# Rows of maxima and factors brought to all partitions by DMA instead of by matmul, and a new order at the heads' end

## What is computed

```python
b = jnp.cumsum(lf, axis=-1)
d_log = jnp.where(causal, b[..., :, None] - b[..., None, :] + ig[..., None, :], -jnp.inf)
inter_log = b + m[..., None]
m_t = jnp.maximum(inter_log, jnp.max(d_log, axis=-1))
dmat = jnp.exp(d_log - m_t[..., None])
inter = jnp.exp(inter_log - m_t)
s = jnp.einsum('bhtd,bhsd->bhts', q, k) * dmat
num = jnp.einsum('bhts,bhsd->bhtd', s, v) + inter[..., None] * jnp.einsum('bhvd,bhtd->bhtv', C, q)
den = jnp.sum(s, axis=-1) + inter * jnp.einsum('bhd,bhtd->bht', n, q)
h = num / jnp.maximum(jnp.abs(den), jnp.exp(-m_t))[..., None]
```

## Time and profile before

| what | us |
|---|---|
| median of 3 runs | 1875.0 (1872.1 to 1875.5) |
| the profiled execution, whole | 1875.4 |
| its span, first to last instruction | 1873.6 |
| TensorE busy (matmuls, modelled ends) | 1829.5 (98%), 9601 matmuls |
| VectorE / ACT / GpSimd busy | 1045.4 / 521.3 / 261.3 |
| DMA moved | 320 MB, 171 GB/s in the mean |

### The profile page before, as it was taken

The page is one execution under the profiler, slowest core; times in us unless marked ns, Lnnn a source line. Parts: engine busy times, 40 slices in busy tenths (PEclk is TensorE's granted clock), DMA queues, the critical chain, the costliest instruction groups (busy, mean ns, idle before and its releaser), DMA issues.

```text
span 1873.6 us, 25258 instructions
## 1 busy us (share of the span) xinstructions
PE 1829.5 (98%) x9601; PEld 1567.2 (84%) x9601; DVE 1045.4 (56%) x2340; ACT 521.3 (28%) x1054; POOL 261.3 (14%) x229
## 2 busy tenths in 40 slices
PE   6989999999999999999999999999999999999998
PEld 5877889888898888988888888888889888898886
DVE  6686774546636276353853447453673627636373
ACT  3344321332223122222222223132221312222221
POOL 3442222030220002000030001200022000210000
PEclk9899999999999999999999999999999999999999
DMA  9885634594256542664427642466425654266421
GB/s 330 269 307 170 208 101 178 166 308 158 90 183 190 175 152 80 214 191 158 135 91 236 192 168 91 149 212 202 147 82 192 189 179 150 76 216 192 137 97 68
DMA packets 134620, 319.94 MB, mean 171 GB/s; under 512 B 11788, under 2 KB 53476, under 8 KB 134500
## 3 DMA queue, kind: packets, MB, share of 16 engines
q1 hardware_dynamic: 129028, 312.56, 50.6%
q10 hardware_dynamic: 5472, 5.77, 0.9%
HBM read 272.09 MB, written 46.20 MB: 170 GB/s over the span
## 4 chain that ended last, share of the span: by engine, by line
PE 77%; DVE 16%; issue 3%; ACT 2%; DMA 1%; POOL 0%; SPq 0%; ACTq 0%; DVEq 0%; POOLq 0%
PE ps_acc L512 20%; PE ps_acc L514 20%; PE ps_acc L513 20%; PE ps_kv L512 2%; PE ps_kv L513 1%; PE ps_kv L514 1%; PE ps_sco L710 1%; DVE sb_shifted L1609 1%; PE ps_num L525 1%; DVE sb_acc_cv L1466 1%; PE ps_num L738 1%; PE ps_kv L742 1%; PE ps_num L737 1%; DVE sb_hm L1466 1%; PE ps_num L512 1%
## 5 line engine op out<-in xcount | busy, mean ns | idle before, releaser
L512 PE MATMUL ps_acc<-sb_hT_hi,sb_w_split 128*128 128x512 f32 x1536 | 603.3, 393 | 1.3 <-POOL sb_w_split L1092 0.7
L514 PE MATMUL ps_acc<-sb_hT_hi,sb_w_split 128*128 128x512 f32 x1536 | 598.8, 390 | 0.0
L513 PE MATMUL ps_acc<-sb_hT_lo,sb_w_split 128*128 128x512 f32 x1536 | 598.8, 390 | 0.0
L514 PEld LDWEIGHTS ps_acc<-sb_hT_hi,sb_w_split 128*128 128x128 f32 x1536 | 288.6, 188 | 61.4
L512 PEld LDWEIGHTS ps_acc<-sb_hT_hi,sb_w_split 128*128 128x128 f32 x1536 | 289.1, 188 | 59.6 <-DVE sb_oz L1486 1.0
L513 PEld LDWEIGHTS ps_acc<-sb_hT_lo,sb_w_split 128*128 128x128 f32 x1536 | 288.9, 188 | 59.2
L1104 POOL TENSOR_TENSOR sb_h_rs<-sb_h_var,sb_mhalf 128x4 f32<-128x4 f32 x32 | 32.4, 1012 | 1028.7 <-DVE sb_h_var L1560 1028.7
L1092 POOL TENSOR_TENSOR sb_w_split<-sb_w_raw,sb_w_split 128x512 fp32r<-128x512 f32 (+1 forms) x64 | 88.7, 1396 | 187.3 <-ACT sb_w_split L823 187.2
L1466 DVE SCALAR_TENSOR_TENSOR sb_acc_cv<-sb_shifted,sb_par,sb_acc_cv 128x512 f32<-128x512 f32 x96 | 76.9, 801 | 61.0 <-ACT sb_acc_cv L962 58.5
L1492 DVE TENSOR_TENSOR sb_oz<-sb_tanh,sb_oz 128x512 f32<-128x512 f32 x32 | 22.2, 693 | 150.4 <-ACT sb_tanh L978 150.4
L512 PE MATMUL ps_acc<-sb_wo_hi,sb_mixm_hi 128*128 128x512 f32 x256 | 103.1, 403 | 0.0
(11 more groups left out here) (233 smaller groups left out, 2929.1 us busy)
## 6 DMA issues: line engine op xcount, KB each, us to landing
sb_w_split<-w_kept SPq DMA_DIRECT2D x328, 512.0 KB, 3.6
sb_w_split<-w_kept SPq DMA_DIRECT2D x56, 520.0 KB, 4.5
w_kept<-sb_w_split SPq DMA_DIRECT2D x40, 512.0 KB, 5.1
sb_x_res<-x SPq DMA_DIRECT2D x34, 512.0 KB, 5.3
sb_w_raw<-w_in SPq DMA_DIRECT2D x64, 256.0 KB, 4.6
out<-sb_qT SPq DMA_DIRECT2D x32, 512.0 KB, 2.9
sb_x_in<-x SPq DMA_DIRECT2D x30, 512.0 KB, 5.3
sb_ada_raw<-w_ada SPq DMA_DIRECT2D x8, 1024.0 KB, 9.7
```

The lines of the kernel that those rows point to most:

```text
L512: pe.matmul(dst, st_hi, mv_hi, start=start, stop=False)
L513: pe.matmul(dst, st_hi, mv_lo, start=False, stop=False)
L514: return pe.matmul(dst, st_lo, mv_hi, start=False, stop=stop)
```

## The change

- `wide_rows`, `m_wide`, `inter_wide`, `chunk_sel`, `head_mask` and the matmuls L713 and L726 go, with the five instructions of setup that filled them.
- ACT stores `m_row` and `inter_row` to a DRAM tensor after t = 6 (`keep_rows`), waits for both stores after t = 8, and loads, for each chunk, 4 rows of 128 (2 KB) to all 128 partitions: `load_m_row(j)` and `load_inter_row(j)`, 256 KB each, into `m_row_all` and `inter_row_all`. The next chunk's are issued once this chunk's were read: the maxima's before the Exp of dmat, the factors' before the tanh of tile zp.
- The transposes of hm go to bro instead of sco.
- The order at the heads' end is new on VectorE and ACT.

```diff
-SCO = {("qk", 0): 1, ("qk", 1): 2, ("hm", 0): 3, ("qk", 2): 4, ("hm", 1): 5, ("qk", 3): 6, ("hm", 2): 7, ("hm", 3): 8}
+SCO = {("qk", j): j + 1 for j in range(NC)}
...
-        m_wide, inter_wide = sb("m_wide", [P, NH, P], F32R), sb("inter_wide", [P, NH, P], F32R)
-        chunk_sel = sb("chunk_sel", [P, NC], F32R)
-        head_mask = sb("head_mask", [16, NH])
+        m_row_all, inter_row_all = sb("m_row_all", [P, BLK]), sb("inter_row_all", [P, BLK])
+        rows_kept = nc.dram_tensor("rows_kept", [2, 16, P], F32, kind="Internal").ap()
...
     heads_to_scores(j), TensorE
-                    bro_wait(5 + 2 * j)
-                    pe.matmul(bro[:, :], col(chunk_sel, j), m_wide[:, :, :].rearrange("p h t -> p (h t)"),
-                              start=True, stop=True).then_inc(bro_full, 1)
...
     numerator_and_update(j), TensorE
-                    pe.wait_ge(bro_free, b * B_USES + (7 + 2 * j))
+                    pe.wait_ge(q_in_ready, b * NC + (j + 1))
...
                 def hm_transposed(j):
-                    pe.wait_ge(sco_free, b * S_USES + SCO["hm", j])
+                    bro_wait(5 + j)
                     pe.wait_ge(hm_ready, b * NC + (j + 1))
                     for h in range(NH):
-                        last = pe.transpose(sco[:, chunk(h)], hm[:, h, :], ident)
-                    last.then_inc(sco_full, 1)
+                        last = pe.transpose(bro[:, chunk(h)], hm[:, h, :], ident)
+                    last.then_inc(bro_full, 1)
...
                     tile("u", j)
                     keys_transposed(j)
-                    inter_rows(j)
                     tile("zp", j)
...
+                def keep_rows():
+                    act.dma_start(rows_kept[0], m_row[0:16, :]).then_inc(rows_kept_done, 16)
+                    act.wait_ge(inter_row_ready, b + 1)
+                    act.dma_start(rows_kept[1], inter_row).then_inc(rows_kept_done, 16)
+
+                def load_m_row(j):
+                    act.dma_start(m_row_all[:, :], rows_kept[0, NH * j:NH * j + NH, :].rearrange("h t -> (h t)").partition_broadcast(P)).then_inc(
+                        m_row_loaded, 16)
...
+                    if t == 6:
+                        keep_rows()
                     if t == 8:
                         exponents()
+                        act.wait_ge(rows_kept_done, 32 * (b + 1))
+                        load_m_row(0)
+                        load_inter_row(0)
...
     chunk j, ACT
-                    act.wait_ge(bro_free, b * B_USES + (6 + 2 * j))
+                    act.wait_ge(m_row_read, b * NC + (j + 1))
+                    if j < NC - 1:
+                        load_m_row(j + 1)
                     act.activation(dmat[:, :, :], dmat[:, :, :], ACT.Exp, scale=-1.0).then_inc(d_exp, 1)
...
                     src, free = acc_wait("zp", j)
+                    act.wait_ge(q_in_ready, b * NC + (j + 1))
+                    if j < NC - 1:
+                        load_inter_row(j + 1)
                     tanh_wait(16 + j)
...
+                y_high(3)
                 squares(3)
-                y_high(3)
...
     chunk j, VectorE
-                    bro_read(5 + 2 * j)
+                    dve.wait_ge(m_row_loaded, 16 * (b * NC + (j + 1)))
...
-                    bro_read(6 + 2 * j)
+                    dve.wait_ge(inter_row_loaded, 16 * (b * NC + (j + 1)))
...
-                    if j >= 2:
-                        m_low(j - 2)
+                    if j == 2:
+                        m_low(0)
...
-                    if j > 0:
+                    if 0 < j < 3:
                         m_mixed(j - 1)
-                    if j >= 2 and not last_block:
-                        prep_scale(b + 1, j - 2)
+                    if j == 2 and not last_block:
+                        prep_scale(b + 1, 0)
...
-                in_turn()
-                step(V.memset(warm[:, :, :], 1.0))
+                if first:
+                    in_turn()
+                    step(V.memset(warm[:, :, :], 1.0))
                 heads(3)
+                y_low(3)
                 update_c(3)
                 head_var(3)
-                y_low(3)
+                m_mixed(2)
+                m_low(1)
                 head_norm(3)
+                if not last_block:
+                    prep_scale(b + 1, 1)
```

More of the change, by code:

```diff
@@ L60 @@
 TANHS = 20
-SCO_FULLS = 8
+SCO_FULLS = 4
 S_USES = 1 + SCO_FULLS
-B_USES = 13
+B_USES = 9
 SLOT = 1152
@@ L242, in build @@
         inter_row_ready, expo_ready, expo_done = sem("inter_row_ready"), sem("expo_ready"), sem("expo_done")
-        rows_lo = sem("rows_lo")
+        rows_kept_done = sem("rows_kept_done")
+        m_row_loaded, inter_row_loaded = sem("m_row_loaded"), sem("inter_row_loaded")
+        m_row_read, q_in_ready = sem("m_row_read"), sem("q_in_ready")
         fold_loaded = [sem("fold_loaded0"), sem("fold_loaded1")]
@@ L1344, in one_block @@
                 count[0] = 0
-                base[0] = b * DVE_STEPS + setup_steps
+                base[0] = b * DVE_STEPS + setup_steps + (not first)
                 def bro_read(u):
@@ L1436, in exponents @@
                     did(expo_ready, b + 1)
-                def wide_rows():
-                    in_turn()
-                    dve.wait_ge(inter_row_ready, b + 1)
-                    for src, wide in ((m_row[0:16, :], m_wide), (inter_row, inter_wide)):
-                        step(V.tensor_tensor(wide[0:16, :, :], src.unsqueeze(1).broadcast_to([16, NH, P]),
-                                             head_mask[:, :].unsqueeze(2).broadcast_to([16, NH, P]), ALU.mult))
-                    in_turn()
-                    for src, wide in ((m_row[0:16, :], m_wide), (inter_row, inter_wide)):
-                        for h in range(NH):
-                            last = V.scalar_tensor_tensor(wide[LO_ROW:LO_ROW + 16, h, :], src, head_mask[:, h:h + 1],
-                                                          wide[0:16, h, :].bitcast(F32), ALU.mult, ALU.subtract)
-                    last.then_inc(rows_lo, 1)
-                    did(rows_lo, b + 1)
                 gates_read()
@@ L1503, in one_block @@
                         exponents()
-                    if t == 8:
-                        wide_rows()
                     if first and t > WOUT_TILE and t - WOUT_TILE <= KT:
@@ L1585, in m_mixed @@
                     in_turn()
-                    dve.wait_ge(sco_full, b * SCO_FULLS + SCO["hm", j])
-                    V.tensor_tensor(oz[:, :, chunk(j)], sco[:, :].rearrange("p (h t) -> p h t", t=P), oz[:, :, chunk(j)],
-                                    ALU.mult).then_inc(sco_free, 1)
-                    did(sco_free, b * S_USES + (SCO["hm", j] + 1))
+                    bro_read(5 + j)
+                    V.tensor_tensor(oz[:, :, chunk(j)], bro[:, :].rearrange("p (h t) -> p h t", t=P), oz[:, :, chunk(j)],
+                                    ALU.mult).then_inc(bro_free, 1)
+                    did(bro_free, b * B_USES + (6 + j))
                 def m_low(j):
@@ L1625, in one_block @@
                     in_turn()
-                    bro_read(5 + 2 * j)
+                    dve.wait_ge(m_row_loaded, 16 * (b * NC + (j + 1)))
                     for h in range(NH):
-                        last = V.scalar_tensor_tensor(dmat[:, h, :], bro[:, chunk(h)], a_pad[:, NH * j + h:NH * j + h + 1],
+                        last = V.scalar_tensor_tensor(dmat[:, h, :], m_row_all[:, chunk(h)], a_pad[:, NH * j + h:NH * j + h + 1],
                                                       bigm, ALU.subtract, ALU.add)
-                    last.then_inc(bro_free, 1)
-                    did(bro_free, b * B_USES + (6 + 2 * j))
+                    last.then_inc(m_row_read, 1)
+                    did(m_row_read, b * NC + (j + 1))
                     in_turn()
@@ L1723, in one_block @@
                 out_norm(3)
-                assert count[0] == DVE_STEPS, count[0]
+                assert count[0] == DVE_STEPS + first, count[0]
             one_block(0, False, True)
```

29 lines of the change are left out of this document (8 added, 21 removed).

## The result

The changed kernel takes 1848.1 us (median of 4 runs, 1847.8 to 1848.9), the kernel before 1875.1 in the runs beside it: a ratio of 0.9861, 95% interval 0.985 to 0.9873. The forecast was 1847.5 us, its range 1844.5 to 1857. The profiled execution took 1848.9 (span 1847.1), 26.5 less than the one before; the forecast against that one was 27.7 less. The sum came out, but its terms are not all the size that the prediction gave them, and what undoing each part costs is another number again.

What follows compares the result with a forecast made beforehand. The order of TensorE's work was taken as the bound. Terms -14.5 - 9.0 - 3.3 - 1.5 + 0.6 = -27.7 us from 1875.4 gave 1847.7, stated as 1847.5 us for the median; range 1844.5 to 1857.

Steps and rivals of the forecast that it cites:

- The 64 products: Row-product matmuls leaving TensorE's queue, two per chunk, would each save one 0.227 us step, all of it path: 14.5 us.
- The bank: With hm's transposes out of the scores' bank, waits at the scores of later chunks would go: 9.0 us, 3.3 in block 0.
- No wait follows there: In their own bank, hm's transposes wait only for VectorE's L1587 of one chunk earlier, so no new wait was expected.
- Heads' end: Before the output's second half, TensorE would no longer wait for y's low half in blocks 1 to 6: 3.3 us.
- wide_rows, 1.5 us less 0.3 in block 0: Removing VectorE's widened rows saves 1.5 us before block 0's fold; ACT's two stores delaying conv copies there cost 0.3.
- The DMAs: The added spread-row loads and their traffic on half-idle engines were taken to cost 0, with a bound of 0 to +3 us.
- The 0.06 for operands in SBUF alone: VectorE's product, now reading only SBUF, would take 0.75 us against 0.69 from PSUM: 0.06 us more each.
- A: Rival: VectorE becomes the bound at the heads' end, 2 us per block return as waits: 1863 us, half gives 1855; chance 0.1.
- C: Rival: spread rows land late, stopping VectorE then TensorE in 24 places; at 18 us landing, 1920 us; chance 0.04.
- B: Rival: removed TensorE matmuls were partly free, each giving back only 0.131 us: 1853.5 us; chance 0.05.
- D: Rival: gaps at TensorE's scores stay because another bank or buffer ends the same wait: 1856.5 us; chance 0.05.
- the 0.6 set aside for costs: Block 0: 0.3 us for ACT's two stores delaying conv copies, 0.3 for possibly no margin left at its heads' end.

Runs made afterwards that it cites:

- the three works ahead: Changed kernel with only m's mixed product and low half of one chunk and the next input's second scaling put back ahead of the last division: 1855.1 us.

## Why the prediction was right, point by point

- **The 64 products, 14.5 us: right**, 14.4 by the ledger (0.45 in each of 32 chunks) and 14.7 when they were put back. But "all of it is path" holds only in company: with the old bank and order 4 to 5 us came out, and of a steady block's 1.8 only 0.6.
- **The bank, 9.0 us: too much, by 2.5.** The ledger gives 0.20 in chunk 2 of eight blocks (1.6; forecast 1.8), and in chunk 3 0.74 in block 2, 0.46 in five blocks, 0.30 in the last (3.3; forecast 3.9 by the earlier trace rows). The step that failed is block 0: 3.3 forecast, 1.6 measured. The wait at the scores went, and its low clock with it (1.00 over 243 to 247 where it was 0.59), but 2.2 us came back one tile later as the wait for the state update. Even the 1.6 has luck in it: behind this new wait the clock stayed up, where two kernels with the same wait lost some 1.6 us to the lower clock. "No wait follows there" looked only at the transposes' own bank, not at the next thing that VectorE's lateness holds.
- **Heads' end, 3.3 us: 4.1**, as block 0's end gained 0.74 too, where 0.3 of cost had been allowed. The waits of the earlier trace rows are gone and transposes to tile is 0.79 as forecast. The margin was put at 1 us and is 1.8. One reason: VectorE had been held by TensorE's L726 (0.33 us in chunk 2 of block 2), which the prediction never read when it called VectorE busy from chunk 1 on.
- **wide_rows, 1.5 us less 0.3 in block 0: 1.63 before the first scores.** The size holds, by other parts: 1.46 at 146 and three waits of 0.41 behind it went, and 0.35 more of stall at 133 and some 0.9 of low clock behind it came (window 140 to 144: 0.84 before, 0.57 after). The forecast had 0.3 for a delay by ACT's two stores; the 0.35 looks like it, but kernels with the stores in the same place have the stall at 4.70 to 5.04 us and the clock at 0.55 to 0.81, so neither figure is shown to be the change's.
- **The DMAs, 0: right.** ACT's issue was 0.33 us in the median, not 0.455, landings 3.1 to 7.6 us. The weights' median landing went from 3.7 to 4.2 us, with nobody waiting: what the Trainium skill says of queues that share their engines (DMA: Bandwidth & Descriptors, Issuing engines are not separate DMA queues) agrees in direction and costs nothing here. The 0.06 for operands in SBUF alone was wrong: 0.692 us against 0.687, the form of the earlier trace rows was the wrong neighbour.
- **The rivals.** A and C did not happen but both were shown to be near: some 2 us more of VectorE's work ahead of a reader begins the first, and a load issued one wait later brings on the second. B is refuted by the added products, D by the waits.

In sum 14.4 + 6.5 + 4.1 + 1.6 = 26.6, where 27.7 was forecast. The closeness is partly luck: the bank gave 2.5 less than forecast, the heads' end 0.8 more, and the 0.6 set aside for costs is not seen in the sum. And adding the terms was right only because all three parts were changed at once.

## What to carry to other kernels

When a second engine runs only a few us behind the bound one (VectorE comes to the last division 3.1 us behind TensorE's state update here, with 1.8 us of margin left at the reader), gains don't add: the loads alone and the order alone gave 4 to 5 us each, all together 27, and taking one part away cost 15 or 23. So price such parts in the final state and by the margins there, and do not judge one by itself. When a stall goes, follow the late engine's queue past the buffer that was freed to the next instruction that someone waits for (the state update here, the next tile's low half in the fold). A row or factor that is known early was better fetched here by a load issued a chunk ahead than by a product in the bound engine's queue, which also ties its reader to that place; issued only behind the chunk's own Exp, it cost four fifths of the gain.

## What was not expected of the hardware

- A load of one 2 KB row of DRAM into all 128 partitions (256 KB) lands in 3.1 to 7.6 us, median 4.4 and 4.7, and holds ACT's issue for 0.33 us. That is longer than the six plain loads of 256 KB on the same queue in block 0 of the kernel before (medians 3.0 and 3.3) and near the 512 KB ones of the weights on SP's queue (4.0 in the median of the page), and early enough here.
- The granted clock after a stall isn't settled by the stall's length: 2.60 us between starts was followed by 1.00 in one kernel, 2.59 by 0.57 in another, at the same place of block 0, and there 3.64 by 1.00 in a third (the three works ahead); and of seven stalls of 1.80 to 1.81 us between starts in the changed kernel with the old order, two (blocks 0 and 4) were followed by seven or eight steps of 0.427, five by none. What else decides stays open.
